# Splitting the first two loads of a float32 decoder-layer kernel and shortening its run of ones products

## What is computed

```python
def mixer_layer(x, mk, mv, conv_buf, h0, g_pre, g_post, w_in, w_out, g_v, w_s, b_s,
                w_conv, b_conv, w_a, b_a, w_x, b_x, lam):
    h = rmsnorm(x, g_pre)
    z = h @ w_in
    u, v, ga, xb, gb, q, gc = jnp.split(z, cuts, axis=-1)
    vn = rmsnorm(v.reshape(n, t, A_HEADS, A_HEAD_DIM), g_v.reshape(A_HEADS, A_HEAD_DIM))
    out_a = chunk_spatial_gate(u.reshape(...), vn, w_s, b_s).reshape(n, t, A_WIDTH)
    out_a = out_a * jax.nn.silu(ga)
    xc, new_buf = causal_conv(xb, conv_buf, w_conv, b_conv)
    hs, h_last = rg_lru(xc, h0, w_a, b_a, w_x, b_x, lam)
    out_b = hs * jax.nn.silu(gb)
    out_c = cross_attend(q, mk, mv) * jax.nn.silu(gc)
    o = jnp.concatenate([out_a, out_b, out_c], axis=-1) @ w_out
    y = x + rmsnorm(o, g_post)
```

## Time and profile before

| | us |
|---|---|
| three runs, median (lowest to highest) | 378.1 (377.32 to 378.69) |
| the profiled execution, whole | 377.31 |
| its span, from first to last instruction | 375.6 |
| PE busy | 367.6 (98%) |
| DVE, ACT, POOL busy | 282.9, 214.4, 146.0 |
| mean granted clock of TensorE | 0.997 |

### The profile page before, as it was taken

The page is one execution under the profiler, slowest core; times in us unless marked ns, Lnnn a source line. Parts: engine busy times, 40 slices in busy tenths (PEclk is TensorE's granted clock), DMA queues, the critical chain, the costliest instruction groups (busy, mean ns, idle before and its releaser), DMA issues.

```text
span 375.6 us, 5744 instructions
## 1 busy us (share of the span) xinstructions
PE 367.6 (98%) x2274; PEld 349.7 (93%) x2274; DVE 282.9 (75%) x362; ACT 214.4 (57%) x371; POOL 146.0 (39%) x86
## 2 busy tenths in 40 slices
PE   8999999999999999999999999999999999999993
PEld 7999889999999999999999989999998899988873
DVE  4998897523668977868757999597399969359596
ACT  6986836853652653674959815944947255203722
POOL 3031771572554323842293066110551994002300
PEclk9999999999999999999999999999999999999998
DMA  7996035611130143424210002603113033030632
GB/s 275 401 392 242 0 114 114 223 58 56 58 112 2 56 121 92 138 70 143 69 58 27 31 9 82 248 21 131 75 47 123 2 112 113 0 117 31 195 113 113
DMA packets 18939, 41.14 MB, mean 110 GB/s; under 512 B 4408, under 2 KB 8800, under 8 KB 18656
## 3 DMA queue, kind: packets, MB, share of 16 engines
q1 hardware_dynamic: 18768, 40.70, 31.4%
q10 hardware_dynamic: 144, 0.08, 0.1%
HBM read 35.90 MB, written 4.87 MB: 109 GB/s over the span
## 4 chain that ended last, share of the span: by engine, by line
PE 69%; DVE 14%; DMA 7%; ACT 4%; issue 3%; SPq 1%; POOL 1%; DVEq 0%; POOLq 0%
PE ps L480 39%; PE ps L739 12%; PE ps L757 6%; DMA mixT<-in_xT 3%; DVE probs L1400 3%; DMA q_rows<-zT 2%; DVE rstdB L1424 2%; PE ps L617 1%; PE ps L684 1%; DMA spread<-q_rows 1%; PE ps L585 1%; DVE zT L1414 1%; PE ps L587 1%; PE ps L606 1%; DVE mixT L1531 1%
## 5 line engine op out<-in xcount | busy, mean ns | idle before, releaser
L480 PE MATMUL ps<-x_hi,w_hi 128*128 128x344 f32 x450 | 145.4, 323 | 0.0
L480 PE MATMUL ps<-x_lo,w_hi 128*128 128x344 f32 x450 | 143.7, 319 | 0.0
L480 PE MATMUL ps<-x_hi,w_lo 128*128 128x344 f32 x450 | 143.7, 319 | 0.0
L480 PEld LDWEIGHTS ps<-x_hi,w_hi 128*128 128x128 f32 x450 | 84.6, 188 | 0.2
L480 PEld LDWEIGHTS ps<-x_lo,w_hi 128*128 128x128 f32 x450 | 84.5, 188 | 0.2
L480 PEld LDWEIGHTS ps<-x_hi,w_lo 128*128 128x128 f32 x450 | 84.5, 188 | 0.0
L1215 POOL TENSOR_TENSOR w_lo<-w_stage,w_hi 128x1024 fp32r<-128x1024 f32 x17 | 42.1, 2479 | 99.4 <-ACT w_hi L827 83.9
L1357 DVE TENSOR_TENSOR zT<-ps,rstdB 128x344 f32<-128x344 f32 x33 | 16.8, 510 | 21.0 <-PE ps L480 20.9
L827 ACT ACTIVATE w_hi<-w_stage 128x1024 fp32r<-128x1024 f32 x17 | 17.8, 1053 | 20.7 <-PE ps L480 20.7
L1323 POOL TENSOR_TENSOR zT<-zT,x_ring 128x1024 f32<-128x1024 f32 x4 | 12.9, 3216 | 36.6 <-DVE zT L1790 36.6
L739 PE MATMUL ps<-x_hi,w_hi 128*128 128x512 f32 x64 | 25.5, 398 | 0.0
(11 more groups left out here) (338 smaller groups left out, 841.3 us busy)
## 6 DMA issues: line engine op xcount, KB each, us to landing
w_stage<-in_w_tiles SPq DMA_DIRECT2D x17, 512.0 KB, 4.0
mixT<-in_xT SPq DMA_DIRECT2D x8, 516.0 KB, 8.7
x_ring<-in_x_all SPq DMA_DIRECT2D x6, 512.0 KB, 4.1
o_y<-zT SPq DMA_DIRECT2D x5, 512.0 KB, 2.9
zT<-in_w_mem SPq DMA_DIRECT2D x4, 512.0 KB, 11.9
cache<-in_kc SPq DMA_DIRECT2D x8, 256.0 KB, 3.2
cache<-in_vcT SPq DMA_DIRECT2D x8, 256.0 KB, 3.1
spread<-p_rows SPq DMA_DIRECT2D x16, 128.0 KB, 3.1
```

The costliest lines, as they stand in the source:

```text
L480: last = pe.matmul(ps[:, bank, 0:GN], w[:, slot, wk], xx[:, k, cols], start=(x == 0 and n == 0), stop=(x == KT - 1 and n == 2))
```

## The change

The load of `w_first` is cut in two. The half for input tile 0 (128 columns of each of the two weight tiles, two runs of 512 bytes per partition) leads the queue. Then come the first 344 columns of input tile 0, its other 688 columns, and the half of `w_first` for input tile 1; the other loads follow in their old order. ACT splits the first weights (2 copies of 128 columns), waits for the first columns of x and splits that group, then the two other groups, then the second half of the weights (2 copies of 128 columns), and goes on with input tile 1. DVE does the low parts in the same new order. PE waits for the second half's low parts ahead of (0,1) and (1,1). `WARM` goes from 11 to 8.

```diff
-WARM = 11
+WARM = 8
...
-            sp.dma_start(w_first, d["w_first"]).then_inc(wfirst_in, 16)
+            sp.dma_start(w_first[:, :, 0:P], d["w_first"][:, :, 0:P]).then_inc(wfirst_in, 16)
             for k in range(KT):
                 if k in (2, 3):
                     sp.dma_start(w_stage[:, k - 2, WF:DM], d["w_tiles"][k - 2, :, WF:DM]).then_inc(w_in[k - 2], 16)
-                sp.dma_start(mixT[:, k, :], d["xT"][:, k, :]).then_inc(ktile_in[k], 16)
+                if k == 0:
+                    sp.dma_start(mixT[:, 0, 0:GN], d["xT"][:, 0, 0:GN]).then_inc(xfirst_in, 16)
+                    sp.dma_start(mixT[:, 0, GN:TT], d["xT"][:, 0, GN:TT]).then_inc(ktile_in[0], 16)
+                    sp.dma_start(w_first[:, :, P:WF], d["w_first"][:, :, P:WF]).then_inc(wsecond_in, 16)
+                else:
+                    sp.dma_start(mixT[:, k, :], d["xT"][:, k, :]).then_inc(ktile_in[k], 16)
...
             def start_tiles(m, k):
+                if k == 1:
+                    pe.wait_ge(wfirstlo_done, m + 3)
...
             for m in range(2):
-                act.activation(w_hi[:, m, 0:WF], w_first[:, m, :], ACT.Copy).then_inc(wfirsthi_done, 1)
+                act.activation(w_hi[:, m, 0:P], w_first[:, m, 0:P], ACT.Copy).then_inc(wfirsthi_done, 1)
             act.wait_ge(par_in, 16)
+            act.wait_ge(xfirst_in, 16)
...
                 for g in range(NG):
                     cols = slice(g * GN, (g + 1) * GN)
+                    if k > 0 or g > 0:
+                        act.wait_ge(ktile_in[k], 16)
                     act.activation(x_hi[:, k, cols], mixT[:, k, cols], ACT.Copy, scale=pc("g_pre", k)).then_inc(xghi_done, 1)
-            for k in range(2):
-                act.wait_ge(ktile_in[k], 16)
-                high_x_groups(k)
+            high_x_groups(0)
+            act.wait_ge(wsecond_in, 16)
+            for m in range(2):
+                act.activation(w_hi[:, m, P:WF], w_first[:, m, P:WF], ACT.Copy).then_inc(wfirsthi_done, 1)
+            high_x_groups(1)
...
-            for m in range(2):
-                dve.wait_ge(wfirsthi_done, m + 1)
-                dve.tensor_tensor(w_lo[:, m, 0:WF], w_first[:, m, :], w_hi[:, m, 0:WF].bitcast(F),
-                                  ALU.subtract).then_inc(wfirstlo_done, 1)
+            def low_first(k):
+                for m in range(2):
+                    cols = slice(k * P, (k + 1) * P)
+                    dve.wait_ge(wfirsthi_done, 2 * k + m + 1)
+                    dve.tensor_tensor(w_lo[:, m, cols], w_first[:, m, cols], w_hi[:, m, cols].bitcast(F),
+                                      ALU.subtract).then_inc(wfirstlo_done, 1)
...
             for k in range(2):
+                low_first(k)
                 low_x_groups(k)
```

More of the change, by code:

```diff
@@ L289, in build @@
         qhi_done = sem("qhi_done")
-        wfirst_in = sem("wfirst_in")
+        wfirst_in, wsecond_in, xfirst_in = map(sem, ("wfirst_in", "wsecond_in", "xfirst_in"))
         sumhi_done, sumlo_done = sem("sumhi_done"), sem("sumlo_done")
```

## The result

The changed kernel takes 379.36 us (median of 7 runs, 378.73 to 379.94), the kernel before 377.84 (7 runs beside it, 377.32 to 378.69). The ratio is 1.0039 with a 95% interval of 1.0029 to 1.0049, so the change makes the kernel slower. The forecast was 378.3 in a range of 377.0 to 379.3, and the measured median lies just above that range. The change costs 1.5 us where the forecast said 0.2. The prediction gave a chance of 0.82 to a difference too small to measure and 0.11 to a kernel that is clearly slower, so that the direction was right earns it little.

The account below looks back on a forecast made before the run. The prediction took the landing of the x loads, through the chain to L606, to set the end: +0.2 us for loads, 0 for PE's earlier start, so the median 378.1 becomes 378.3, range 377.0 to 379.3.

Parts of the forecast that it names:

- part 3: Loads of x and weights: smaller packets delay the last input tile, +0.2 us, bounds 0 to 0.8.
- The high bound: Loads: short packets at 72 ns as at start-up, 0.7 us for the first half, 0.8 with the second.
- the full stretch: Load queue running full, 3 to 5 us: small packets 27 ns each there, the reason for taking 0.2 us.
- The cover for SP's later issues: Ahead of input tile 1: 772 KB, 2 us of work, hide its 0.9 us later issue; uncovered, up to 0.9.
- Part 1: First product with x: PE starts at 5.25 us, 1.1 us earlier, as fewer bytes stand ahead of it.
- Part 2: PE's head start turns into waits of 0.1 to 0.6 us at (0,1), (1,2), (0,4); the rest is worth nothing.
- The chain through L606: Second attention scores: PE waits 0.23 us for POOL, traced through the queries' DRAM round trip to tile 7's landing; +0.2 us.
- Part 4: Ones products ahead of the first x product: eight cost 0 if the clock rises at 4.9 us as before.
- Rival C: x products from 5.25 us: TensorE stays at its lower clock, 0.29 not 0.157 us each; 380.1 if until 12.5; chance 0.09.
- B: PE's start: the 1.1 us head start survives, 377.0; chance 0.06, shared with a shorter round trip.
- A: Attention scores at L606: PE arrives last and counts, -0.25 to 0 us, 378.0; chance 0.18.
- D: Loads at start-up: packets cost 0.8 us, 378.9, or 379.8 with SP's issues uncovered; chance 0.09.

Follow-up runs that it names:

- e11: Kernel before with two 1 KB transfers issued by SP between input tiles 0 and 1: 377.40 against 377.34, ratio 1.0008.
- e6: Kernel before with w_first still one transfer, but read from a padded array as 512 packets of 512 bytes: 377.63 against 377.18, ratio 1.0016.
- e4: Kernel before with only w_first in two, input tile 0 whole between the halves, 11 ones products: 378.35 against 377.02, ratio 1.0036.
- e5: Changed kernel with the first weights stored by input tile, each half one run of 1024 bytes per partition: 377.80 against 377.02, ratio 1.0022.
- e3: Kernel before with only input tile 0's load in two (344 and 688 columns): 377.55 against 377.02, ratio 1.0011.
- the mended ones: Three kernels with the changed kernel's weight halves in 1024-byte runs, the second behind input tile 1; two also move a POOL query step: 377.50, 377.88, 378.23.
- e9: Kernel before with the second query chunk's low part made ahead of the first two key products on POOL: 376.60 against 377.18, ratio 0.9988.
- e10: Changed kernel with the second query chunk's low part made ahead of the first two key products on POOL: 378.56 against 377.18, ratio 1.0045.
- e2: Changed kernel with 11 ones products in place of 8: 378.85 against 377.02, ratio 1.0055.
- e13: The e9 kernel with 8 ones products in place of 11: 378.11; 4 of 12 runs at 376.57 to 376.81, 8 at 378.00 to 378.39.
- e7: The e5 kernel with the second half of the weights issued by ACT behind par, not by SP: 378.43 against 377.18, ratio 1.0032.

## Why the prediction was right in its direction and wrong in its size

**The step that failed is part 3, the term "what the loads cost".** It said +0.2 us, bounds 0 to 0.8; the trace shows 1.64 on tile 7, past the 1 us that the prediction itself had named as the sign of being wrong. It counted the packets right (384 more of the weights, 128 more of tile 0), and it priced them right: 27 ns each, where 27 to 30 were measured. What failed is that this price was taken for the whole cost. Behind the short packets the engines stood idle for a quarter of the time and long packets took twice their time, 160 GB/s from 5.0 to 6.5 us where there had been 391, while input tile 1 was already issued. The high bound had the wrong mechanism too. It took 72 ns for a short packet at start-up, and they took 27 to 30 there. With all 32 weight packets of an engine it would have given 32 x 72 - 8 x 83 = 1.6 us, the measured number, by accident. The sentence that "most of these packets lie in the full stretch" holds for the second half at most: 256 of the 512 belong to the first half, which stands at the head of the queue.

**The cover for SP's later issues.** The prediction reckoned 0.46 us an issue and tile 1 issued 0.9 us later; it was issued 1.54 later (3.25 for 1.71), because SP takes 0.70 and 0.56 us to issue the two halves. e11 shows that 0.9 is covered. The further 0.6 were not tried by themselves.

**What the experiments tell of the cause.** e6 (packets, no further transfer: +0.4 on tile 7), e4 (both halves, +1.0), e5 (half the packets, +0.9) and e3 (tile 0 in two, 0) show that cutting up the weights is what delays the loads, that the short runs have a part in it and are not all of it, and that two transfers with tile 0 between them cost more than one. Cutting tile 0 as well delays tile 7 only where the weights are cut too (+1.6 for e4's +1.0). The landings with the loads of the kernel before were 16.9 to 17.3 (four kernels), with those of the changed one 18.7 to 19.1 (three), with the mended ones 17.6 to 18.2 (three).

**Part 1 was right where it looked.** The first product came at 5.11 for a forecast of 5.25. Its last sentence put the second weights at 5.8; they landed at 2.65 + 4.4 = 7.1. It did not ask when input tile 1 comes, which landed at 9.2 and not at 6.9, and for that PE waited 1.6 us.

**Part 2 had the mechanism.** The chain through L606 passed on what the loads lost, with the longer wait there that was forecast (0.6 for 0.2), and e9 shows that the chain binds. The new wait at (0,1) was forecast at 0.1 to 0.6 us and was 1.6, and (0,4) started 1.54 late, not within 0.2 of its old time. So PE was late by the same 1.5 us on its own, and the chain isn't the only way by which late loads reach the end (e10). What the head start would be worth with loads that come in time, no run shows cleanly; e3 starts PE 0.6 us sooner and is no faster.

**Part 4** gave the ones products a cost of 0 in the changed kernel, and e2 bears it out, if only between sessions: with 11 of them it isn't faster. In the profile the x products at 5.56 to 6.42 are 0.29 us apart, so the clock did rise later than at 4.9, but PE came to the wait of 1.6 us early in any case. Rival C had the mechanism and its price right (0.29 for 0.157), and e13 shows it at work in a kernel whose gap is longer. Rivals B and A found no support. D's mechanism, a short packet that takes 72 ns at start-up, did not happen; only its direction did.

**What stays open.** Why the engines idle and long packets take longer behind short ones: whether descriptors are made or read too slowly, or the data come late, no view here shows. Why e5, with 256 packets of 1024 bytes in two transfers, is later than e6 with 512 of 512 in one. What costs e3 its 0.5 us and e7 its runs above 378. And how much of the changed kernel's scatter is its clock: a rise or fall in an execution that wasn't profiled isn't seen.

## What to carry to other kernels

A small piece of a load, cut out so that work can begin sooner, can be paid by everything behind it: look at the GB/s of the first microseconds, slice by slice, and at the landing of the last tile, not only at that of the first. The time that a short packet holds an engine is not its cost; here that was 27 ns, and the loss lay in idle engines and slow long packets behind it. A number that comes out right by a row with the wrong mechanism (72 ns) proves nothing: read the row again in the kernel after. And ask what the engine meets after its early start: here PE began 1.25 us sooner and stood 1.6 us at the next input tile.

## What the runs showed of the hardware that had not been expected

- The first transfer took SP 0.39 us to issue with 128 runs, 0.70 with 256 runs of 512 bytes and 0.69 with 512 of them (e6); the second half took 0.56, and two tiny transfers 0.43 each (e11).
- A 512-byte packet held a DMA engine for 27 ns, at start-up too (e6, 0 to 3 us). Behind 256 of them the long packets took some 330 ns where they had taken some 150 (estimates; changed kernel, 5.0 to 6.5 us).
- Transfers issued 0.9 us later cost nothing (tile 7 at 16.9), while 512 packets of 512 bytes in place of 128 of 2048, in one transfer at the head, cost 0.45 us (e6; tile 7 was 0.4 late, no more than its scatter).
- After 8 ones products (3.8 us) and a gap of 1.1 us, TensorE ran x products at its lower level to 9.8 us in 8 of 12 executions by their times; after 11 products, 4.1 us in the profiled execution, and the same gap (e9, on another chip), in none of 11.
- The granted clock fell from the upper to the lower level at 11.3 us, after PE had idled 2.3 us up to 10.8, and came back at 14.7 (e2); the products between were 0.29 us apart.
